# Recurrent stage of a two-block network: decays as products of gates, 32x32 near blocks, and another order of the first loads and of the dense work

## What is computed

```python
forget = lb + (1.0 - lb) * jax.nn.sigmoid(f32)
log_f = jnp.log(jnp.maximum(forget, TINY))
k = (1.0 - lb) * jax.nn.sigmoid(-f32)
...
    b = jnp.cumsum(gb, axis=2)
    diff = b[:, :, :, None, :] - b[:, :, None, :, :]
    decay = jnp.where(causal, jnp.exp(jnp.where(causal, diff, 0.0)), 0.0)
    scores = jnp.einsum('bhtd,bhsd,bhtsd->bhts', qb, kb, decay)
```

## Time and profile before

| | |
|---|---|
| median of 3 runs | 1832.29 us (1831.8 to 1834.77) |
| profiled execution: its own time, its span | 1828.68 us, 1826.9 us |
| mean granted TensorE clock | 0.965 of full speed |
| busy: PE, PEld, DVE, ACT, POOL | 1710.2, 1574.1, 1208.1, 901.7, 70.3 us |
| first mixer, from the start to the next layer's first transpose | 0 to 216.97 us |

### The profile page before, as it was taken

How to read it: one execution, slowest core, us unless ns; L and a number is a source line. 1 busy time by engine, 2 the same in 40 slices (tenths; PEclk the granted TensorE clock), 3 DMA queues, 4 the chain that set the end, 5 groups by cost and what they waited for, 6 DMA issues and landing times.

```text
span 1826.9 us, 31495 instructions
## 1 busy us (share of the span) xinstructions
PE 1710.2 (94%) x11510; PEld 1574.1 (86%) x11510; DVE 1208.1 (66%) x1996; ACT 901.7 (49%) x1420; POOL 70.3 (4%) x103
## 2 busy tenths in 40 slices
PE   4888899999889999899989998999899998989998
PEld 4778799989669999899978988999789998689997
DVE  4798587775857777755574876556665656556655
ACT  4543565554356555644355545444553435364433
POOL 0223000000210000000000000000000000000000
PEclk9999999999799999999999999999999999799999
DMA  6532466674325656766647554666456664227662
GB/s 184 160 101 85 139 196 188 180 184 116 95 70 161 192 179 188 223 184 185 193 133 215 187 171 153 191 186 181 138 172 188 178 190 139 69 88 212 179 189 79
DMA packets 390475, 294.00 MB, mean 161 GB/s; under 512 B 22773, under 2 KB 362372, under 8 KB 389892
## 3 DMA queue, kind: packets, MB, share of 16 engines
q1 hardware_dynamic: 387540, 280.83, 52.0%
q0 software_dynamic: 2304, 9.99, 1.6%
q10 hardware_dynamic: 560, 2.23, 0.3%
HBM read 291.93 MB, written 1.07 MB: 160 GB/s over the span
## 4 chain that ended last, share of the span: by engine, by line
PE 67%; DVE 5%; ACT 1%; issue 1%; POOL 0%; DVEq 0%; ACTq 0%
PE ps L375 21%; PE ps L376 21%; PE ps L377 21%; DVE w_lo L366 1%; PE ps L431 1%; PE ps L1155 1%; DVE H L534 1%; PE ps L1689 1%; PE ps L1688 1%; ACT L511 0%; DVE SQ L527 0%; PE ps L1418 0%; ACT SQ L506 0%; DVE A L1336 0%; PE ps L1174 0%
## 5 line engine op out<-in xcount | busy, mean ns | idle before, releaser
L375 PE MATMUL ps<-x_hi,w_hi 128*128 128x256 f32 x2672 | 763.1, 286 | 14.7 <-DVE x_lo L458 6.4
L376 PE MATMUL ps<-x_hi,w_lo 128*128 128x256 f32 x2672 | 759.8, 284 | 0.0
L377 PE MATMUL ps<-x_lo,w_hi 128*128 128x256 f32 x2672 | 759.3, 284 | 0.0
L366 DVE TENSOR_TENSOR w_lo<-raw,w_hi 128x1024 fp32r<-128x1024 f32 x534 | 660.1, 1239 | 42.5 <-ACT w_hi L359 42.0
L359 ACT ACTIVATE w_hi<-raw 128x1024 fp32r<-128x1024 f32 x534 | 543.7, 1046 | 99.8 <-PE ps L377 78.7
L375 PEld LDWEIGHTS ps<-x_hi,w_hi 128*128 128x128 f32 x2672 | 516.5, 193 | 22.1 <-issue 15.5
L376 PEld LDWEIGHTS ps<-x_hi,w_lo 128*128 128x128 f32 x2672 | 516.5, 193 | 4.4
L377 PEld LDWEIGHTS ps<-x_lo,w_hi 128*128 128x128 f32 x2672 | 516.2, 193 | 0.0
L644 ACT ACTIVATE sl<-gs 128x256 f32<-128x256 f32 x88 | 36.9, 419 | 397.8 <-DVE gs L748 397.8
L748 DVE TENSOR_TENSOR gs<-ps,R 128x256 f32<-128x256 f32 x88 | 37.3, 424 | 277.0 <-PE ps L377 277.0
L375 PE MATMUL ps<-w_hi,h_hi 128*128 128x512 f32 x528 | 207.1, 392 | 1.3 <-DVE h_lo L672 1.3
(11 more groups left out here) (243 smaller groups left out, 1482.1 us busy)
## 6 DMA issues: line engine op xcount, KB each, us to landing
raw<-in_ffn_w_up SPq DMA_DIRECT2D x176, 512.0 KB, 3.8
raw<-in_ffn_w_down SPq DMA_DIRECT2D x132, 512.0 KB, 4.3
raw<-in_ffn_w_gate SPq DMA_DIRECT2D x88, 512.0 KB, 4.7
raw<-in_hgrn_w_in SPq DMA_DIRECT2D x32, 512.0 KB, 4.9
raw<-in_gmlp_w_in SPq DMA_DIRECT2D x32, 512.0 KB, 4.4
raw<-in_gmlp_w_out SPq DMA_DIRECT2D x16, 512.0 KB, 4.2
raw<-in_dsa_w_in SPq DMA_DIRECT2D x13, 512.0 KB, 4.5
raw<-in_hgrn_w_out SPq DMA_DIRECT2D x8, 512.0 KB, 4.1
```

The costliest lines, as they stand in the source:

```text
L366: nc.vector.tensor_tensor(w_lo[:, s, :], raw[:, s, :], w_hi[:, s, :].bitcast(F32), ALU.subtract)\
L375: pe.matmul(o, whi, xhi, start=first, stop=False, skip_group_check=not group)
L376: pe.matmul(o, wlo, xhi, start=False, stop=False, skip_group_check=not group)
L377: return pe.matmul(o, whi, xlo, start=False, stop=last, skip_group_check=not group)
```

## The change

- The sum of logs, the exponentials, and POOL's part go. `decays` multiplies neighbouring gates: the decay over 2h tokens is the product of two over h. `widen` then multiplies the later half of each block pair of q, and the earlier half of k, in place by one such decay, so q and k fit the next level.
- For h up to 16 (levels 0 to 5) PE computes only the diagonal blocks of 32x32, each at its own `tile_position`: 64 products per level with 32 weight columns and 32 moving columns, into one PSUM bank. DVE masks one 128x512 tile per level. Level 6 has 32 such products, level 7 has 16 of 64x64, level 8 has 8 of 128x128. ACT copies the results into `Pd`.
- PE's order: one value chunk and one level, eight times, then the gate chunks between the last level, outputs and transposes, then the projection.
- First loads: ACT's queue takes the 64 KB identity, x, then the other constants (0.42 MB). SP takes one small vector load and then goes straight to weights; the 16 other vector loads go to POOL's queue and are transposed after the third chunk. ACT splits one chunk, not four, ahead of L442. Angles and sines move into the projection.

```diff
 HG = 8
-LEVELS = [0, 1, 2, 4, 8, 16, 32, 64, 128]
+NEAR = [0, 1, 2, 4, 8, 16]
...
-        lf, kk, qq, bb = (cut(2 * n * K1, 8, L) for n in range(4))
-        Vh, Gh, Z0 = cut(8 * K1, 2, D), cut(10 * K1, 8, L), cut(12 * K1, 8, L)
+        lf, kk, qq, Qd = (cut(2 * n * K1, 8, L) for n in range(4))
+        Vh, Gh, Fg = cut(8 * K1, 2, D), cut(10 * K1, 8, L), cut(12 * K1, 8, L)
...
+        on = [cut(6 * K1, 2, 512), cut(7 * K1, 2, 512)]
...
+        near_mask = lambda n: col(cst, CC["level"] + n * BLK, BLK).unsqueeze(1).broadcast_to([P, TB * HG, BLK])
...
+        decay = {1: Fg}
+        at_ = 0
+        for h_ in (2, 4, 8, 16, 32, 64):
+            decay[h_] = SQ[:, :, :].rearrange("p a b -> p (a b)")[:, at_:at_ + HG * L // h_].rearrange("p (a n) -> p a n", a=HG)
+            at_ += HG * L // h_
...
+        def ready(n, g):
+
+            return S("hg_up"), (g + 1 if n == 1 else 2 + 4 * (n - 2) + 2 * (g + 1))
...
+            pe.wait_ge(S("in_ident"), 16)
+            pe.wait_ge(S("in_gain0"), 16)
+            pe.transpose(ps[:, 0, 0:16], vst[0:16, 0, :], c_ident[0:16, 0:16]).then_inc(S("vec_ps"), 1)
             pe_turn(pe, "hg")
...
+                if t == 2:
+                    pe.wait_ge(S("in_vec"), 16 * VDMAS[0])
+                    for n in range(VSTAGES):
+                        mm = pe.transpose(ps[:, 5, n * P:n * P + P], vst[:, n, :], c_ident)
+                    mm.then_inc(S("vec_ps"), 1)
+
+            def score(n, g):
+
+                Q = qq if n == 0 else Qd
+                if n == 0:
+                    pe.wait_ge(S("hg_k"), 4 * g + 4)
+                    pe.wait_ge(S("hg_fq"), 13 + 3 * g)
+                else:
+                    pe.wait_ge(*ready(n, g))
+                if n in (2, 3, 4, 5, 7):
+                    pe.wait_ge(S("hg_pred"), min(n - 1, 5))
+                if n == 8:
+                    if g == 0:
+                        pe.wait_ge(S("hg_pred"), 6)
                     else:
...
+                        pe.wait_ge(S("hg_pd"), 6)
+                for hd in range(4 * g, 4 * g + 4):
+                    if n == 8:
+                        mm = pe.matmul(ps[:, 1 + g, (hd % 4) * P:(hd % 4) * P + P], kk[:, hd, 0:P], Q[:, hd, P:L], start=True, stop=True)
+                        continue
+                    for tb in range(TB):
+                        if n < 6:
+                            o = (tb * HG + hd) * BLK
+                            for j in range(4):
+                                t = slice(tb * P + BLK * j, tb * P + BLK * j + BLK)
+                                mm = pe.matmul(ps[BLK * j:BLK * j + BLK, n % 2, o:o + BLK], kk[:, hd, t], Q[:, hd, t],
+                                               start=True, stop=True, tile_position=(0, BLK * j))
+                        elif n == 6:
+                            o = (tb * HG + hd) * BLK
+                            for m in range(2):
+                                a = tb * P + 64 * m
+                                mm = pe.matmul(ps[64 * m:64 * m + 32, 2, o:o + 32], kk[:, hd, a:a + 32], Q[:, hd, a + 32:a + 64],
+                                               start=True, stop=True, tile_position=(0, 64 * m))
+                        else:
+                            a = tb * P
+                            mm = pe.matmul(ps[0:64, (3, 0)[tb], hd * 64:hd * 64 + 64], kk[:, hd, a:a + 64], Q[:, hd, a + 64:a + P],
+                                           start=True, stop=True)
+                mm.then_inc(S("hg_sc"), 1)
+
+            def value_rows(k):
+                c = c0 + 16 + k
+                pe.wait_ge(lo_done, c + 1)
+                if k == 0:
+                    pe.wait_ge(S("vec_own"), 1)
+                    pe.wait_ge(*once("r_done", "hg"))
+                tok_rows(pe, 4, c, k, KT).then_inc(used, 1)
+
+            def gate_tile(t):
+                c = c0 + 24 + t
+                pe.wait_ge(lo_done, c + 1)
+                if t < 2:
+                    pe.wait_ge(S("hg_pd"), 7 + t)
+                else:
+                    pe.wait_ge(S("hg_g"), t - 1)
+                feat_tile(pe, ps[:, (3, 0)[t % 2], 0:L], c).then_inc(used, 1)
 
...
+            for n in range(8):
+                value_rows(n)
+                for g in range(2):
+                    score(n, g)
+            gate_tile(0)
+            for g in range(2):
+                score(8, g)
+            gate_tile(1)
+            gate_tile(2)
             outputs(0)
+            gate_tile(3)
+            outputs(1)
+            gate_tile(4)
+            gate_tile(5)
             turns(0)
-            outputs(1)
-            project(0)
+            gate_tile(6)
+            gate_tile(7)
             turns(1)
-            for g in (1, 2, 3):
-                project(g)
+            for j in range(8):
+                project(j)
...
+            act.dma_start(c_ident, T["constants"][:, CC["ident"]:CC["ident"] + P]).then_inc(S("in_ident"), 16)
             act.dma_start(H[:, :, :], T["x"][0].rearrange("(b p) d -> p b d", p=P)).then_inc(S("in_x"), 16)
+            act.dma_start(cst[:, P:CCOLS], T["constants"][:, P:CCOLS]).then_inc(S("in_cst"), 16)
             act.dma_start(pos_i[:, :], T["positions_2"].broadcast_to([P, L])).then_inc(S("in_pos"), 16)
-            for c in range(HI_AHEAD):
+            act.wait_ge(S("vec_ps"), 1)
+            nc.scalar.activation(vec[:, 0:16], ps[:, 0, 0:16], ACT.Copy).then_inc(S("gain0"), 1)
+            split_hi(act, 0)
+            act.wait_ge(S("gain0"), 1)
+            act_turned(act, "hg", lambda j: ("attn_norm", j), 0)
+            for c in range(1, HI_AHEAD):
                 split_hi(act, c)
...
+            def sigmoids(g):
+                hd = slice(4 * g, 4 * g + 4)
+                act.wait_ge(S("hg_fq"), 4 * g + 4)
+                nc.scalar.activation(flat(Fg[:, hd, :]), flat(lf[:, hd, :]), ACT.Sigmoid).then_inc(S("hg_sig"), 1)
+                nc.scalar.activation(flat(kk[:, hd, :]), flat(lf[:, hd, :]), ACT.Sigmoid, scale=-1.0).then_inc(S("hg_sig"), 1)
+
+            def bounded(g):
+                act.wait_ge(S("lb_done"), 1)
+                act.wait_ge(S("hg_sig"), 2 * g + 2)
+                for j in range(4 * g, 4 * g + 4):
+                    nc.scalar.activation(Fg[:, j, :], Fg[:, j, :], ACT.Identity, scale=lbt[:, 3, j:j + 1], bias=lbt[:, 2, j:j + 1])\
+                        .then_inc(S("hg_F"), 1)
+                for j in range(4 * g, 4 * g + 4):
+                    nc.scalar.activation(kk[:, j, :], kk[:, j, :], ACT.Copy, scale=lbt[:, 3, j:j + 1]).then_inc(S("hg_k"), 1)
...
+                if t == 1:
+                    act.wait_ge(S("vec_ps"), 2)
+                    nc.scalar.activation(vec[:, 16:VSTAGES * P], ps[:, 5, 16:VSTAGES * P], ACT.Copy).then_inc(S("vec_own"), 1)
+                    act.wait_ge(S("lb_z"), 1)
+                    nc.scalar.activation(lbt[:, 1, :], lbt[:, 0, :], ACT.Exp).then_inc(S("lb_e"), 1)
+                if t == 5:
+                    sigmoids(0)
+                if t == 6:
+                    bounded(0)
+                if t == 9:
+                    sigmoids(1)
                 if t == 10:
-                    act.wait_ge(S("hg_fg"), 1)
...
+            for n in range(8):
+                split_hi(act, c0 + 16 + n + HI_AHEAD)
+                if n == 6:
+                    act.wait_ge(S("pd_zero"), 1)
+                    act.wait_ge(S("hg_pred"), 6)
+                    for j in range(4):
+                        t = slice(BLK * j, BLK * j + BLK)
+                        nc.scalar.activation(Pd[t, :, :, t].rearrange("p a b c -> p (a b) c"), Pn[t, :, :], ACT.Copy)\
+                            .then_inc(S("hg_pd"), 1)
+                if n == 7:
+                    act.wait_ge(S("hg_sc"), 14)
+                    for m in range(2):
+                        nc.scalar.activation(Pd[64 * m:64 * m + 32, :, :, 64 * m + 32:64 * m + 64].rearrange("p a b c -> p (a b) c"),
+                                             ps[64 * m:64 * m + 32, 2, :].rearrange("p (a c) -> p a c", c=32), ACT.Copy)\
+                            .then_inc(S("hg_pd"), 1)
+            act.wait_ge(S("hg_sc"), 16)
+            for tb in range(TB):
+                nc.scalar.activation(Pd[0:64, tb, :, 64:P], ps[0:64, (3, 0)[tb], :].rearrange("p (a c) -> p a c", c=64), ACT.Copy)\
+                    .then_inc(S("hg_pd"), 1)
+            split_hi(act, c0 + 24 + HI_AHEAD)
+            act.wait_ge(used, c0 + 24)
+            act.wait_ge(*once("row_r", "hg"))
+            for b in range(4):
+                nc.scalar.activation(Vh[:, b // 2, (b % 2) * 512:(b % 2) * 512 + 512], ps[:, 4 + b, :], ACT.Copy,
+                                     scale=r_tok[:, b // 2:b // 2 + 1]).then_inc(S("hg_v"), 1)
             for hg in range(2):
...
             roots(0)
+            split_hi(act, c0 + 27 + HI_AHEAD)
+            roots(1)
+            split_hi(act, c0 + 28 + HI_AHEAD)
+            silu(0)
+            for t in (5, 6, 7):
+                split_hi(act, c0 + 24 + t + HI_AHEAD)
```

(78 more changed lines are left out.)

291 lines of the change are left out of this document (69 added, 222 removed).

## The result

The changed kernel took 1777.07 us in the median of four executions (1769.84 to 1777.13), the kernel before 1832.76 (1831.80 to 1834.77): ratio 0.9685, 95% interval 0.9659 to 0.9711. The prediction said 1802 (1784 to 1826); the kernel is faster than its range. The profiled execution is the one of 1769.84 us.

What follows compares the result with a forecast made beforehand. PE's order was taken as the bound, with DVE bounding the levels. Start, f and q, levels and end summed to 187.1 us instead of 216.97, saving 29.9: 1828.68 - 29.9 + 3.6 = 1802.4 us, range 1784 to 1826.

Steps and rivals of the forecast that it cites:

- Start: First loads: x lands at 9.2 us, first dense product at 11.7, chunk 2 at 21.3 instead of 36.9.
- chunk 0's own load, split and remainder fit in: At the start: chunk 0's load, issued near 1.5 us instead of 13.80, and its preparation would not delay the first product.
- Vectors on POOL: Sixteen vector loads at 0.8 us each, landed by 23 us: cost 0, or 5 us if weights hold them up.
- f and q: The stage making f and q, with other engines' work hidden, ends at 63.6 us instead of 78.7.
- DVE in a level: Products, one masked copy and a remainder take DVE 4.6 us per level, where it was a full 10.
- The narrow pair: PE in the levels: a weight load plus matmul of 32 columns costs 0.05 us; 832 pairs take 41.6 us.
- End: Gate chunks, level 8, outputs, transposes, projection and two short waits after the levels: 56.0 us, ending at 187.1.
- The rest: Everything behind the first mixer's projection: every later stage keeps its old length.
- that rule: The Trainium skill's rule that products at different column positions run side by side, three of them 2.38 times as fast.
- rival 1: Narrow pairs in the levels are cheap, 0.028 to 0.04 us: total 1784 to 1795 us; chance 0.15.
- Rival 2: PE's clock falls in the levels: 17 to 22 us more, total 1819 to 1825; chance 0.28.
- Rival 3: A narrow pair costs 0.112 us: 52 us more, total 1854; chance 0.10, shared with unseen causes.

Runs made afterwards that it cites:

- a0: The changed kernel run again unedited, to see its spread; median 1775.08 us.
- a1: The changed kernel run again unedited, as control in the rounds of w1, w3 and w2; median 1771.11 us.
- a2: The changed kernel run again unedited, as control for a second run of w3; median 1774.70 us.
- e1: Changed kernel with the near levels' loop over four column positions outermost, so eight products in a row share one position; 1782.95 us.
- e4: Changed kernel with all seven remaining gate chunks ahead of the outputs, then outputs, transposes and projection one behind the other; 1785.38 us.
- f1: Changed kernel with levels 0 to 5 interleaved by quarters: three 512-column value products, then 32 narrow pairs, four times; 1775.54 us.
- v2: Changed kernel with the quarter interleaving of f1 and four gate chunks moved into levels 0, 2, 3 and 5; 1776.89 us.
- w2: w3 with the narrow groups in halves, half a value chunk or a gate ahead of each half; 1774.21 us.
- v1: Changed kernel with three gate chunks moved into levels 0, 2 and 4, ahead of their narrow products; 1774.92 us.
- w3: w1 with three gate chunks moved into levels 0, 2 and 4; 1768.82 us, and 1772.17 us when run again.
- w1: Changed kernel with the norm's squares, root and spread ahead of the first dense product, and identity transposes keeping PE at work early; 1773.29 us.
- g1: Changed kernel with weight chunks 24 to 33, issued during the levels, loaded for one partition only, so work is left out; 1770.91 us.
- e2: Changed kernel with every near product issued twice, 768 more pairs in the same order of positions; 1797.52 us.
- s2: Changed kernel with weight chunks held until x has landed, and identity transposes keeping PE at work while it waits for x; 1778.57 us.

## Why the prediction was wrong

By its own steps, for the profiled execution:

- *Start.* x at 9.2: 8.85. First dense product 11.7: 14.34. Chunk 2 at 21.3: 23.7, 2.4 late. The step "chunk 0's own load, split and remainder fit in" failed: the load landed at 11.48, and the scaling is queued behind its split. No wait of 1.1 at the spread came, since PE was late itself; in a0, a1 and a2 it did come.
- *Vectors on POOL.* Cost 0: right. They were issued at 0.51 us each, done at 9.6, and PE transposed them at 26.49 without a wait.
- *f and q.* End 63.6: 64.6, no gap. 41.5 us for 14 chunks.
- *DVE in a level,* 4.6: 4.28 from start to start, near. But "DVE is no longer the bound unless PE needs under 4.6" came true in its second half: PE needs some 4.35, so the two engines are level.
- *The narrow pair* is the failed step: 0.05 us, measured 0.0105. 768 x 0.05 = 38.4 became 6 x 1.4 = 8.4, the change of shape behind each group included; level 6 1.2 instead of 3.2; level 7 2.1 instead of 1.8. The levels with their value chunks took 37.0 instead of 67.5: 30.5 of the 30.9 us between 187.1 and 156.17. The reason given for 0.05, load, stream and issue one behind the other, does not hold: even neighbours in one position take 0.026 (e1), and four positions in turn 0.0105. The prediction's estimate by the Trainium skill (TensorEngine Tiling (Array Packing), Instruction Overhead), 21 us for the 832 pairs, fits e1's price (832 x 0.026 = 21.6) and not the change's.
- *End.* 56.0: 54.6, with waits of 0.77 and 0.58 for the forecast 0.9 and 0.6. e4 shows that the cover was real.
- *The rest* kept its length within the spread: 1611.8 us behind the stage end, 1609.9 before, 1609.9 to 1615.8 in a0, a1 and a2.

That PE's time per narrow pair sets the levels was right, the size of that one term was not. The range's low end failed with it. Its lower bound for a pair, 0.028, is what e1 measures for neighbours in one position, 0.026; the change puts neighbours in four. The prediction had that rule beside rival 1, and wrote that it "would end near the same place, since DVE's 4.6 and the value chunk come next". It was not worked out: with pairs of 0.011 a level goes by DVE's 4.6 us instead of the 2.75 + 3.6 of rival 1, six levels are 10 us shorter, and rival 1's 1784 becomes 1774. Rival 2 (narrow tiles lower the clock) didn't come: 1.00 in every window of the levels in the profile after. The clock did fall for one value chunk each in a0 and a1, but behind a stop and not through the tiles. Rival 3 (0.112) didn't come either. What no case had: 1.2 to 6.0 us of stops for instructions, seen in a0, a1, a2 (3.4, 1.9) and the profile after. They make the usual execution slower than the profiled one, and so bring the median nearer to the forecast: 25.3 us below it, where the profiled execution is 28.9 below the 1798.8 of its own sum. That it came nearer is luck. Without stops the levels would be near what DVE allows.

Open: the rest of the program behind the first mixer took 1609.9 to 1617.8 us in the profiled executions, whatever the variant; the granted clock of the second block's windows differs a little between them, but was not traced to its cause. Whether the pages are bound by rate or by burst is not settled either. The versions that cut the narrow groups in parts (f1, v2, w2) had 0 to 0.2 us of stops, below every execution of the changed kernel. Gate chunks between whole groups show no clear effect: v1 had 3.0, w3 0.8 and 0.7, and w1 without them 1.3.

## What to carry to other kernels

Price small matmuls by where neighbours lie: with output rows of 32 in four column positions in turn, a pair cost 0.0105 us, in one position 0.026, whole 128x128 tiles 0.11. When a bound of a range rests on work one behind the other, work out the case side by side too, down to the engine that is next. And count instructions against time: where 256 of them lasted 4.4 or 1.7 us beside weight loads (a0), PE stopped with "issue" in the middle of a group, and where they lasted 4.7 (f1), it did not. The instruction queue in the DMA view shows the pages. Cutting the groups in parts with dense work between them removed the stops, but each change of shape took back a part of the gain.

## What the runs showed of the hardware that I had not expected

- From the beginning of one 16 KB page of PE's instructions to the next went 5.2 us where weight packets delayed it (a0), 3.1 without weight loads (g1) and 2.8 with them but out of their way (the profile after). Stops were 1.2 to 6.0 us from one execution to another of the same kernel, 16.0 with doubled pairs (e2).
- A change between 128x512 products and 32x32 ones cost 0.13 us (f1).
- An idle stretch of PE can cost more than its own length: the value chunk behind the stop of 3.64 us ran at 0.50 of the clock and took 2.3 us longer (a0).
- The first dense products went at 0.21 us from start to start until 20.4 us, 0.12 after, though the profile after has a granted clock of 1.00 in both stretches. The kernel before has the same two steps with 0.50 and 1.00 beside them, so the first 1.00 is most likely a gap in the record. First the profile after, then two windows of the kernel before:

```profile
14.30:20.20 5.90, 5.86 (x27) 5.89 (x28) 4.90 (x9) 5.86 (x10) 3.95 (x14) 1.00 1.18 274
```

```profile
26.50:31.00 4.50, 4.46 (x21) 4.49 (x22) 4.33 (x14) 4.48 (x10) 0.00 (x0) 0.50 1.20 290
31.50:34.00 2.50, 2.50 (x23) 2.50 (x22) 2.30 (x8) 2.45 (x4) 0.00 (x0) 1.00 0.04 10
```

- With PE at work from 2.99 us on (s2) the products went at 0.12 from the first one.
